# Opening of a fused decoder layer: order of the first loads, and norm steps placed among the angle steps

## What is computed

```python
h = rms_norm(x, norm1_g[l])
qa, ka, va, qb, kb, vb, gb, gate_a, gate_b = jnp.split(h @ w_in[l], split_idx, axis=-1)
qa = apply_rope(rms_norm(qa..., q_norm_g[l]), positions, ROPE_DIM, ROPE_THETA)
ka = apply_rope(rms_norm(ka..., k_norm_g[l]), positions, ROPE_DIM, ROPE_THETA)
...
# rms_norm: x * rsqrt(mean(x * x) + 1e-6) * g
# apply_rope: ang = positions * freqs; cos(ang), sin(ang)
```

## Time and profile before

| | us |
|---|---|
| median of 3 runs | 1493.64 |
| lowest and highest | 1492.24, 1494.34 |
| span of the profiled execution, first to last instruction | 1487.5 |
| TensorE busy | 1425.9 (96%) |
| VectorE busy | 1007.2 (68%) |
| ScalarE busy | 828.2 (56%) |

### The profile page before, as it was taken

The page is one execution under the profiler, slowest core; times in us unless marked ns, Lnnn a source line. Parts: engine busy times, 40 slices in busy tenths (PEclk is TensorE's granted clock), DMA queues, the critical chain, the costliest instruction groups (busy, mean ns, idle before and its releaser), DMA issues.

```text
span 1487.5 us, 19516 instructions
## 1 busy us (share of the span) xinstructions
PE 1425.9 (96%) x7296; PEld 1200.9 (81%) x7297; DVE 1007.2 (68%) x1443; ACT 828.2 (56%) x1342; POOL 405.7 (27%) x462
## 2 busy tenths in 40 slices
PE   5899999999999999999999969999999999999995
PEld 5788888888888788888888858888888888888874
DVE  6855664664674623344332557999999999999994
ACT  5653453353353323233233237888888888888881
POOL 2225424424433400000000110233333333333331
PEclk9999999999999999999999979999999999999998
DMA  6010110210210143363340549999999999999991
GB/s 219 23 44 15 47 43 1 61 43 1 61 44 0 56 116 85 85 174 100 85 176 9 219 151 402 373 386 387 391 385 387 385 391 394 390 396 390 392 351 42
DMA packets 134032, 286.39 MB, mean 193 GB/s; under 512 B 18864, under 2 KB 97840, under 8 KB 109360
## 3 DMA queue, kind: packets, MB, share of 16 engines
q1 hardware_dynamic: 119216, 263.79, 49.1%
q0 software_dynamic: 13248, 21.00, 3.8%
q10 hardware_dynamic: 1472, 0.32, 0.1%
HBM read 287.16 MB, written 25.17 MB: 210 GB/s over the span
## 4 chain that ended last, share of the span: by engine, by line
PE 87%; DVE 3%; DMA 3%; ACT 2%; POOL 2%; issue 1%; POOLq 0%; DVEq 0%; ACTq 0%
PE proj L105 17%; PE proj L107 16%; PE proj L106 16%; PE scores L105 6%; PE scores L107 6%; PE scores L106 6%; DMA w_slot<-in_w_up 2%; PE outs L757 2%; PE scores L690 2%; PE scores L568 2%; PE turned L105 1%; PE turned L107 1%; PE turned L106 1%; PE outs L848 1%; PE turned L568 1%
## 5 line engine op out<-in xcount | busy, mean ns | idle before, releaser
L1725 DVE TENSOR_TENSOR w_low<-w_slot,w_high 128x2048 fp32r<-128x2048 f32 x192 | 430.6, 2283 | 1.1 <-ACT w_high L1168 1.0
L1168 ACT ACTIVATE w_high<-w_slot 128x2048 fp32r<-128x2048 f32 x190 | 351.8, 1906 | 19.0 <-DMA w_slot<-in_w_up 7.8
L105 PE MATMUL proj<-w_high,xeH 128*128 128x512 f32 x512 | 203.8, 398 | 4.0 <-DVE xeL L1828 1.9
L107 PE MATMUL proj<-w_high,xeL 128*128 128x512 f32 x512 | 200.5, 392 | 0.0
L106 PE MATMUL proj<-w_low,xeH 128*128 128x512 f32 x512 | 200.1, 391 | 0.0
L1356 POOL DMA_INDIRECT out<-y,ids_rows x32 | 87.5, 2735 | 353.7 <-DVE y L1838 353.7
L981 ACT ACTIVATE wCH<-wC_in 128x1024 fp32r<-128x1024 f32 x48 | 47.6, 1052 | 153.5 <-DMA wC_in<-in_w_branch_b 153.5
L1420 DVE TENSOR_TENSOR wCL<-wC_in,wCH 128x1024 fp32r<-128x1024 f32 x48 | 56.9, 1237 | 91.9 <-ACT wCH L981 91.9
L105 PEld LDWEIGHTS proj<-w_high,xeH 128*128 128x128 f32 x512 | 96.9, 189 | 25.5 <-issue 3.4
L107 PEld LDWEIGHTS proj<-w_high,xeL 128*128 128x128 f32 x512 | 96.5, 189 | 20.9
L106 PEld LDWEIGHTS proj<-w_low,xeH 128*128 128x128 f32 x512 | 96.7, 189 | 19.2
(11 more groups left out here) (289 smaller groups left out, 3155.0 us busy)
## 6 DMA issues: line engine op xcount, KB each, us to landing
w_slot<-in_w_gate SPq DMA_DIRECT2D x64, 1024.0 KB, 10.1
w_slot<-in_w_up SPq DMA_DIRECT2D x64, 1024.0 KB, 10.0
w_slot<-in_w_down SPq DMA_DIRECT2D x64, 1024.0 KB, 10.2
wC_in<-in_w_in SPq DMA_DIRECT2D x32, 512.0 KB, 4.9
wB_in<-in_w_in SPq DMA_DIRECT2D x16, 512.0 KB, 6.3
wA_in<-in_w_in SPq DMA_DIRECT2D x12, 512.0 KB, 6.0
x_all<-in_x SPq DMA_DIRECT2D x4, 1024.0 KB, 9.2
wC_in<-in_w_branch_a SPq DMA_DIRECT2D x16, 256.0 KB, 5.6
```

The costliest lines, as they stand in the source:

```text
L105: pe.matmul(out, lh, rh, start=start, stop=False)
L107: return pe.matmul(out, ll, rh, start=False, stop=stop)
L1168: act.activation(w_high[slot][:], w_in6[slot][:], ACT.Copy).then_inc(S["w_split"], 1)
L1725: dve.tensor_tensor(w_low[slot][:], w_in6[slot][:], w_high[slot][:].bitcast(F32), ALU.subtract).then_inc(S["w_lows"], 1)
```

## The change

SyncE issues its loads before the 16 increments. The pair of tiles 0 and 1 becomes two loads, with the gain row between them; tile 1 has a semaphore of its own, `x_next`. Of the three loads of `wA_in`, the one of the K columns moves to ScalarE's queue. The two loads of `gains` move from there to SyncE's queue, behind its two loads of `wA_in` and the increments. On VectorE the mean of tile 0 stands before the first of the three turn products, and norm of tile 0 and mean of tile 1 behind it; norm of tile 1 stands behind all angle steps. On ScalarE the high half of turned tile 0 stands before the sine.

```diff
         @block.sync
+            sp.dma_start(x_all[:, 0, :], x_v[:, 0, :]).then_inc(S["x_in0"], DMA)
+            sp.dma_start(g1_row[:], T["norm1_g"][0].partition_broadcast(P)).then_inc(S["g1_in"], DMA)
+            sp.dma_start(x_all[:, 1, :], x_v[:, 1, :]).then_inc(S["x_next"], DMA)
+
+            def load_A(head, first=False):
+                for j, col in enumerate((QA, KA, VA)):
+                    if first and j == 1:
+                        continue
+                    sp.dma_start(wA_in[:, :, 128 * j:128 * j + 128],
+                                 w_in_v[:, :, DS(head * 128 + col, 128)]).then_inc(S["wA_landed"], DMA)
+
+            load_A(0, first=True)
             for name in STARTS_FREE:
                 sp.sem_inc(S[name], FREE)
-            sp.dma_start(x_all[:, 0:2, :], x_v[:, 0:2, :]).then_inc(S["x_in0"], DMA)
-            sp.dma_start(g1_row[:], T["norm1_g"][0].partition_broadcast(P)).then_inc(S["g1_in"], DMA)
...
-            load_A(0)
+            for j, n in enumerate(("q_norm_g", "k_norm_g")):
+                sp.dma_start(gains[:, j, :], T[n][0].partition_broadcast(P)).then_inc(S["gains_in"], DMA)
...
-            for j, n in enumerate(("q_norm_g", "k_norm_g")):
-                act.dma_start(gains[:, j, :], T[n][0].partition_broadcast(P)).then_inc(S["gains_in"], DMA)
+            act.dma_start(wA_in[:, :, 128:256], w_in_v[:, :, KA:KA + 128]).then_inc(S["wA_landed"], DMA)
 
             def square_tile(i):
-                act.wait_ge(S[f"x_in{i // 2}"], DMA)
+                act.wait_ge(S["x_next" if i == 1 else f"x_in{i // 2}"], DMA)
...
             square_tile(0)
             square_tile(1)
+            high_tile(0)
             act.wait_ge(S["consts_in"], DMA)
             act.wait_ge(S["ang_step"], 9)
             act.activation(sin_t[:], ang[:], ACT.Sin).then_inc(S["trig_done"], 1)
             act.activation(cos_t[:], turns[:], ACT.Sin, scale=-1.0, bias=const("half_pi")).then_inc(S["trig_done"], 1)
-            high_tile(0)
...
-            for part in TWO_PI:
+            mean_tile(0)
+            angle(dve.scalar_tensor_tensor(ang[:], turns[:], -TWO_PI[0], ang[:], ALU.mult, ALU.add))
+            norm_tile(0)
+            mean_tile(1)
+            for part in TWO_PI[1:]:
                 angle(dve.scalar_tensor_tensor(ang[:], turns[:], -part, ang[:], ALU.mult, ALU.add))
             angle(dve.tensor_scalar(ang[:], ang[:], PI_BELOW, -PI_BELOW, ALU.min, ALU.max))
             angle(dve.scalar_tensor_tensor(turns[:], ang[:], -1.0, ang[:], ALU.mult, ALU.max))
-            for i in range(2):
-                mean_tile(i)
-            for i in range(2):
-                norm_tile(i)
+            norm_tile(1)
             low_tile(0)
```

More of the change, by code:

```diff
@@ L373, in x_bank @@
             return bank(2 * half + (1 if i else 0))
-        names = """pos_in late_in g1_in consts_in gains_in small_in x_in0 x_in1 x_in2 x_in3 x_sq_done x_ms_done x_rstd_done
+        names = """pos_in x_next late_in g1_in consts_in gains_in small_in x_in0 x_in1 x_in2 x_in3 x_sq_done x_ms_done x_rstd_done
             xn_done xT_done hH_done hL_done lam_step ang_step trig_done
@@ L444, in _ @@
         def _(sp):
+            sp.dma_start(x_all[:, 0, :], x_v[:, 0, :]).then_inc(S["x_in0"], DMA)
[8 more added lines that the diff above has]
+            load_A(0, first=True)
             for name in STARTS_FREE:
                 sp.sem_inc(S[name], FREE)
-            sp.dma_start(x_all[:, 0:2, :], x_v[:, 0:2, :]).then_inc(S["x_in0"], DMA)
-            sp.dma_start(g1_row[:], T["norm1_g"][0].partition_broadcast(P)).then_inc(S["g1_in"], DMA)
-            def load_A(head):
-                for j, col in enumerate((QA, KA, VA)):
-                    sp.dma_start(wA_in[:, :, 128 * j:128 * j + 128],
-                                 w_in_v[:, :, DS(head * 128 + col, 128)]).then_inc(S["wA_landed"], DMA)
-            load_A(0)
+            for j, n in enumerate(("q_norm_g", "k_norm_g")):
+                sp.dma_start(gains[:, j, :], T[n][0].partition_broadcast(P)).then_inc(S["gains_in"], DMA)
             for j in (1, 2, 3):
```

## The result

The changed kernel takes 1497.55 us (median of 4 runs, 1497.11 to 1498.25), the kernel before beside it 1493.14 (1492.24 to 1494.34). The two medians are 4.4 us apart (1.0030). The recorded ratio is 1.0042, interval 1.0028 to 1.0056, or 6.3 us of 1491 (4.2 to 8.3); the interval holds both. So the kernel is slower by some 4 to 8 us, where 1495.1 and no measurable difference were forecast. The range of 1492.6 to 1497.0 doesn't hold it.

What follows compares the result with a forecast made beforehand. TensorE, busy 96% of the span, was taken as the bound, so its first projection's start counts: 12.05 + 8.2 = 20.25 instead of 18.79, +1.5 us. Span 1489.0 plus 6.1 gives 1495.1 us, range 1492.6 to 1497.0.

Steps and rivals of the forecast that it cites:

- SyncE's earlier issue: In the opening, SyncE issues its first load as early as ScalarE, near 0.75 instead of 1.71: 0.96 us earlier.
- The increments cost nothing: SyncE's 16 increments, run behind its loads near 9 us, are waited on only after 18.79: cover about 10 us.
- When tile 1 lands: Second token tile in the opening: lands at 12.05 us, bounds 8.9 and 14.5, with break-even at 10.6.
- The rule weighed in the prediction: DMA engines take queues in turn by 9 to 17 descriptors, so nearly all of K would pass ahead of tile 1.
- Rival 2: K load gets ahead of tile 1 on the shared DMA engines: +3.0 to +3.9 us, 1497.0 taken; chance 15%.
- rival 1: Tile 1 lands by 10.6 or sooner; TensorE starts where before or earlier, 1492.9 or 1492.6 us; chance 23%.
- The chain from tile 1: From tile 1's landing through square, mean, angle steps, sine, cosine and w_in's high half to first projection: 8.2 us.
- t1: The moment token tile 1 lands in the opening, taken as 12.05 us.
- I carry a later or earlier start one to one to the end: Any shift of TensorE's first projection start, here +1.5 us, reaches the kernel's end in full.
- The tables' cover of 6.4 us: GpSimd's tables end at 19.42 and VectorE reads them at 25.82, so moving the gains loads costs nothing.
- TensorE's clock: First projections ran at a slow pace; a longer slow stretch costs 1.5 us; no mean, only a wider range.
- The sum: Span 1487.5 + 1.5 = 1489.0, plus 6.1 us for start and end around the span, gives 1495.1.

Runs made afterwards that it cites:

- e1: The changed kernel with the 16 semaphore increments put back ahead of SyncE's loads, nothing else; 1494.53 us against 1491.24, ratio 1.0024.
- e6: The changed kernel with the positions' load moved from ScalarE's queue to the head of SyncE's queue, ahead of tile 0; 1494.10 us, ratio 1.0025.
- e7: The changed kernel with the positions' load at the head of SyncE's queue and VectorE's and ScalarE's orders of before; 1490.77 us against 1491.01, ratio 0.9997.
- e3: The changed kernel's new loads with the old orders of steps on VectorE and ScalarE; 1495.12 us, ratio 1.0026.
- e5: e1 with one added wait: GpSimd's tables held until VectorE has made all low halves of w_in; 1494.59 us in one run.
- e13: The kernel before with one tiny VectorE copy (128x8) behind the absolute value of the angle; 1491.03 us, ratio 0.9995.

## Why the prediction was wrong, point by point

**SyncE's earlier issue: right** (0.76; 0.75 said). **The increments cost nothing: right** where they stand; no wait for them shows from 8 to 40 us. What they did was not looked at: they had kept SyncE's loads 0.96 behind ScalarE's, and so the positions ahead of the token rows.

**The failed step: "When tile 1 lands. This decides the case."** What decided was the landing of the positions. The prediction priced each moved load and each queue, but started the angle steps where they had started before, at 4.00, since the positions' own line was not touched; they started at 10.35. They are 1024 pieces of 4 bytes, issued on ScalarE's queue at 1.20, now behind the first token rows at 0.76. Issues with their us to landing, before and changed:

```profile
consts<-in_consts ACTq DMA_DIRECT2D x1, 244.5 KB, 2.8
posi<-in_positions ACTq DMA_DIRECT2D x1, 4.0 KB, 2.8
```

```profile
x_all<-in_x SPq DMA_DIRECT2D x2, 512.0 KB, 5.7
...
consts<-in_consts ACTq DMA_DIRECT2D x1, 244.5 KB, 4.9
posi<-in_positions ACTq DMA_DIRECT2D x1, 4.0 KB, 9.1
```

And packets, MB and share of the engines by queue, changed kernel, 5.4 to 8.5 us and then 8.5 to 10.3:

```profile
q1 hardware_dynamic: 637, 1.03, 93.0%
q10 hardware_dynamic: 614, 0.00, 11.1%
```

```profile
q1 hardware_dynamic: 660, 0.33, 76.5%
q10 hardware_dynamic: 667, 0.13, 47.4%
```

q1 is SyncE's queue, q10 ScalarE's. The two moved packet for packet, 637 to 614 and 660 to 667, and so each 4-byte piece waited for a packet of SyncE's queue (1.6 KB in the mean, 1.03 MB by 637). The rule weighed in the prediction (the Trainium skill, page "DMA: Bandwidth & Descriptors", section "Queues, rings and completion order": 9 to 17 descriptors from one queue before the next) speaks of larger turns. These counts alone can't show the size of one turn. Equal shares do agree with turns of one size for both queues; that K's pieces would then pass many at a time for each token row was a misreading of the rule. Nor is every stretch equal (e1, 493 to 187). Rival 2 was not put to the test in the changed kernel: ScalarE's queue moved 0.00 MB from 5.4 to 8.5, so K still stood behind the positions when tile 1 landed.

**The landing itself: mis-sized.** 12.05 was said, 8.47 measured, rival 1's case: tile 0 landed 4.6 us after issue and tile 1 6.8. It brought nothing, since the angle was later still.

**The chain from tile 1: right in size, wrong in what heads it.** From t1 to the first projection are 7.96 in e1 and 7.96 in e6 (10.78 to 18.74). In the changed kernel it is headed by the angle: 10.35 and then 11.35 to the start. The steps between mean and norm now cost as foreseen, an engine in order, with norm 0 (13.74 to 15.02) and its 0.58 wait for GpSimd in the middle of the angle's chain, where the prediction had it hidden.

**"I carry a later or earlier start one to one to the end": wrong.** Beside TensorE runs VectorE's line: eight low pieces of w_in, the low half of tile 1, the mean and norm of tile 2 and the steps behind them, for which TensorE stands still 1.26 us at 31.30 already before. The earlier trace rows and the rows at 22.10 and 31.30 were there to be read. The table has every case: e7 starts 1.3 earlier and gains 0.5 on that line, e3 starts 3.7 later and loses 4.0.

**The tables' cover of 6.4 us: right as to who reads them, wrong in "nothing".** Moving them onto VectorE's low pieces cost 1.15 us, and e5 shows that it is they.

**TensorE's clock: no part of the shift between these two profiles.** Length, busy of each engine, granted clock and so on, before and changed:

```profile
32.00:36.00 4.00, 3.42 (x13) 3.38 (x12) 3.27 (x13) 1.95 (x7) 1.82 (x3) 0.57 0.96 265
```

```profile
32.00:36.00 4.00, 2.40 (x21) 1.99 (x19) 3.15 (x8) 1.72 (x6) 0.40 (x1) 1.00 0.00 0
36.00:40.00 4.00, 3.42 (x14) 3.32 (x13) 3.27 (x13) 2.01 (x8) 1.81 (x3) 0.64 0.94 262
```

The stretch near 1.2 GHz moved with the work by 4 us and kept its length: 3.4 us before, and 3.4 after with 0.93 from 40 to 44. The slow pace of the first projections (0.32 us each) is another matter: the granted clock is 1.00 there in both profiles (20 to 22 and 22 to 24 us), so the prediction's tie of that pace to the clock has no row for it.

**The sum: a wrong 6.1.** It took the profiled execution of before (1487.5) for a typical one. An execution takes 2.1 more than its span, so that one took about 1489.6, quicker than the medians of the kernel before in the four later sets of runs (1491.24, 1491.01, 1490.93, 1491.74). This only blurred the base; it doesn't explain the miss.

**The gather: not foreseen at all.** No step of the prediction looked past the opening for places where two engines start within 0.13 us of each other.

**The chances.** "Slower" got 0.15, with the K load as its mechanism. The mechanism that came, a small untouched load behind a large one that was moved up, was on nobody's list.

## What to carry to other kernels

When a large load is issued earlier, list every load that was in flight at that time and not only those the diff names: one of many tiny pieces is hit hardest, and it may head the longest chain. Price an opening by following each engine's own line until all have met a later common point, here the second tile, rather than by the first matmul. And where two engines start within a tenth of a microsecond of each other on work that gets in each other's way, any change upstream can turn their order, so that its effect is found hundreds of microseconds away.

## What the runs showed of the hardware that was not expected

- In the changed kernel two queues that shared the DMA engines moved equal numbers of packets of unlike size (637 to 614, 660 to 667), though in e1 once 493 to 187. A load of 1024 four-byte pieces took 9.1 us behind SyncE's 4 KB rows. Issued ahead of them it took 2.8 or 3.2 (before, e1), and 5.2 in e13 with the loads of before.
- GpSimd's indirect DMA issue took 1.32 us when it started 0.12 to 0.13 ahead of VectorE's 2.28 us subtraction, and 3.35 when it started as much behind, in nine profiles alike; the subtraction took 2.28 either way. The page "SBUF — State Buffer" of the Trainium skill, section "Who interferes with whom", says that issue order decides who blocks, which these rows bear out. It also infers that a subtraction of two tensors (tensor_tensor) leaves descriptor writing alone. Here the issue was held; whether in writing descriptors or in reading ids_rows, the traces do not say.
- VectorE's low pieces of w_in and GpSimd's tables slow each other: eight pieces 3.84 to 5.24 us, the tables 3.7 to 6.05. One after the other they would take 7.5; side by side both were done in 6.05.
- The stretch at half of the full clock near 32 to 44 us lasted 0, 3.4 or 6.8 us from profile to profile, and moved all that follows by up to 1.4 us.
- VectorE stalls 0.28 us at one instruction (counts_f) in some programs and not in others. TensorE's matmul, whose result it reads, was done by 882.75 (before, start 882.38, 0.37 long), so that wait does not explain it.
